# One ring of seven buffers for the experts' weights, and a new order of a short stretch of the plan

## What is computed

```
h   = x * (1 + scale1) + shift1
branches A (convolution), B (top-k attention), C (chunked gating), each projected to 1024
x   = LN(alpha*x + (1+gate1) * (merged @ w_o))
h2  = x * (1 + scale2) + shift2
scores = sigmoid(h2 @ w_router);  2 experts per token, inside one group of 4
for e in 16 experts:
    he = silu(h2 @ w_e_gate[e]) * (h2 @ w_e_up[e])      # 1024 -> 512, twice
    y += gate_e * (he @ w_e_down[e])                    # 512 -> 1024
out = LN(alpha*x + (1+gate2) * y)
```

## Time and profile before

| | us |
|---|---|
| median of 3 runs | 1103.73 |
| lowest and highest | 1097.69, 1103.95 |
| the profiled execution | 1103.72 |
| its span, first to last instruction | 1101.7 |
| PE busy | 1004.7 (91%) |
| DVE busy | 488.5 (44%) |
| mean granted TensorE clock | 0.952 |

### The profile page before, as it was taken

The page is one execution under the profiler, slowest core; times in us unless marked ns, Lnnn a source line. Parts: engine busy times, 40 slices in busy tenths (PEclk is TensorE's granted clock), DMA queues, the critical chain, the costliest instruction groups (busy, mean ns, idle before and its releaser), DMA issues. The chain is left out here.

```text
span 1101.7 us, 22153 instructions
## 1 busy us (share of the span) xinstructions
PE 1004.7 (91%) x8966; PEld 672.6 (61%) x8966; DVE 488.5 (44%) x1277; ACT 189.6 (17%) x447; POOL 247.5 (22%) x281
## 2 busy tenths in 40 slices
PE   4999999999899999999999999987999999998940
PEld 3777778456676667677777764565555555555520
DVE  1122999972357788855104005677133011110117
ACT  1110112113121213221111110111111111111103
POOL 0000004536121123222335410000221221111133
PEclk8998999999898999999999999977999999999975
DMA  9964645442514206114081317143969899999856
GB/s 293 306 124 144 196 154 173 175 159 100 212 29 153 64 29 194 31 45 115 11 199 49 115 48 306 67 181 111 354 254 414 332 375 393 419 404 423 349 151 127
DMA packets 93732, 214.23 MB, mean 194 GB/s; under 512 B 23464, under 2 KB 48303, under 8 KB 89533
## 3 DMA queue, kind: packets, MB, share of 16 engines
q1 hardware_dynamic: 78388, 186.20, 47.4%
q0 software_dynamic: 6400, 19.01, 5.8%
q10 hardware_dynamic: 8849, 7.64, 2.6%
HBM read 200.46 MB, written 16.92 MB: 197 GB/s over the span
## 5 line engine op out<-in xcount | busy, mean ns | idle before, releaser
L1765 PE MATMUL bank<-arena 128*128 128x288 f32 (+6 forms) x1778 | 443.0, 405 | 5.4 <-issue 2.1
L1765 PEld LDWEIGHTS bank<-arena 128*128 128x128 f32 (+2 forms) x1778 | 320.8, 192 | 119.5 <-issue 44.7
L2156 PE MATMUL bank<-arena 128*32 128x256 f32 x3136 | 180.6, 381 | 9.2 <-issue 7.1
L2156 PEld LDWEIGHTS bank<-arena 128*32 128x32 f32 x3136 | 102.7, 109 | 79.1 <-issue 12.3
L1717 DVE TENSOR_TENSOR arena<-arena,bank 128x128 f32<-128x128 f32 x49 | 14.2, 289 | 230.7 <-ACT arena L1154 230.5
L917 POOL DMA_INDIRECT expert_rows<-arena,ints x49 | 47.7, 974 | 228.6 <-ACT arena L1165 228.6
L2175 PE MATMUL bank<-arena 128*32 128x256 f32 x1568 | 95.8, 385 | 0.0
L867 POOL TENSOR_SCALAR arena<-arena 128x288 f32<-128x288 f32 x46 | 43.2, 938 | 209.2 <-ACT arena L1107 209.2
L1227 DVE SCALAR_TENSOR_TENSOR arena<-arena 128x512 f32<-128x512 f32 x120 | 81.9, 741 | 0.0
L1779 PE MATMUL bank<-arena 128*128 128x288 f32 x256 | 69.0, 427 | 2.6 <-DVEq L1245 2.6
L1769 PE MATMUL bank<-arena 128*128 128x128 f32 (+7 forms) x315 | 51.2, 297 | 17.3 <-DMA arena<-constants 5.3
(11 more groups left out here) (284 smaller groups left out, 891.4 us busy)
## 6 DMA issues: line engine op xcount, KB each, us to landing
arena<-in_w_e_gate SPq DMA_DIRECT2D x16, 2048.0 KB, 11.9
arena<-in_w_e_up SPq DMA_DIRECT2D x16, 2048.0 KB, 17.1
arena<-in_w_e_down SPq DMA_DIRECT2D x16, 2048.0 KB, 22.2
arena<-in_w_ada SPq DMA_DIRECT2D x8, 2048.0 KB, 10.3
arena<-in_w_in SPq DMA_DIRECT2D x8, 2048.0 KB, 10.0
arena<-in_w_ada SPq DMA_DIRECT2D x8, 1024.0 KB, 11.6
arena<-in_x_prompt SPq DMA_DIRECT2D x8, 512.0 KB, 7.3
arena<-in_w_in SPq DMA_DIRECT2D x14, 256.0 KB, 8.3
```

What stands on the lines that cost most here:

```text
L1765: last = pe.matmul(out, a, b, start=k == 0, stop=k == len(pairs_) - 1)
L2156: last = pe.matmul(out, HG[:, g % 2, k, a:a + BLK], gate_up[i % 2][:, :, k, c * P:c * P + P], start=k == 0, stop=k == KT - 1)
```

## The change

Two things change.

First, the seven buffers become one ring. Load number n = 3i + y (y = 0 gate, 1 up, 2 down) goes to slot n % 7 and may be issued when load n - 7 has been used: `room` waits for `dn_full` when that one was a down, for `hid_full` when it was a gate or up, and for `weights_up` when the slot had none. So the gate of expert i takes the slot of the down of expert i - 3, and the up and down of expert i take those of the gate and up of expert i - 2. The DMAs, their sizes and their number stay the same. The gate and up of an expert now lie any distance apart, and where up lies below gate the two halves of the PSUM bank are swapped (`gate_half`, `up_half`). Of the first loads, the down of expert 0 and the gate of expert 1 are issued where the gate and up of expert 1 were; the down of expert 1 goes early, its up late.

Second, a stretch of the plan is reordered.

```diff
-    plan += [("lnA1", 2), ("lnA2", 1), ("nat", "u", 4), ("mix", 0), ("ada", 11), ("lnA1", 3), ("lnA2", 2), ("mix", 1), ("mix", 2), ("lnA1", 4), ("lnA2", 3)]
-    plan += [("yc", 0), ("mix", 3), ("lnA2", 4), ("yc", 1), ("yc", 2)]
+    plan += [("lnA1", 2), ("lnA2", 1), ("nat", "u", 4), ("lnA2", 2), ("lnA1", 3), ("mix", 0), ("ada", 11), ("lnA1", 4), ("lnA2", 3), ("mix", 1), ("mix", 2)]
+    plan += [("lnA2", 4), ("yc", 0), ("mix", 3), ("yc", 1), ("yc", 2)]
...
-    down_ring = [ring[2], ring[5], V(A_DOWN3, SLOT)]
+    SLOT_AT = [A_RING2, A_RING2 + SLOT] + [A_RING + k * SLOT for k in range(3)] + [A_RING2 + 2 * SLOT, A_DOWN3]
+    RING = len(SLOT_AT)
+    slots = [V(a, SLOT) for a in SLOT_AT]
+    loaded = lambda n: (ev(f"w_in{n % RING}"), 16 * (n // RING + 1))
...
+    up_first = lambda i: SLOT_AT[3 * i % RING] > SLOT_AT[(3 * i + 1) % RING]
+    gate_half = lambda i: slice(P, 2 * P) if up_first(i) else slice(0, P)
+    up_half = lambda i: slice(0, P) if up_first(i) else slice(P, 2 * P)
+    def both_weights(i, k, c):
+        lo, hi = sorted((SLOT_AT[3 * i % RING], SLOT_AT[(3 * i + 1) % RING]))
+        return bass.AP(slots[0].tensor, lo + 512 * k + P * c, [[A_END, P], [hi - lo, 2], [1, P]])
+    def room(eng, n):
+        if n < RING:
+            eng.wait_ge(ev("weights_up"), 1)
+        else:
+            j, y = divmod(n - RING, 3)
+            eng.wait_ge(ev("dn_full" if y == 2 else "hid_full"), FIRST[j + 1])
...
             if t == 1:
-                expert_weights(sp, 0, 0)
-                expert_weights(sp, 0, 1)
-                expert_down(sp, 0, 0)
+                expert_weights(sp, 0, 0, 0)
+                expert_weights(sp, 0, 1, 1)
+                expert_down(sp, 1, 5)
...
         sp.wait_ge(slot_out, rel[("wo", 1)])
-        expert_weights(sp, 1, 3)
-        expert_weights(sp, 1, 4)
+        expert_down(sp, 0, 2)
+        expert_weights(sp, 1, 0, 3)
...
         sp.wait_ge(ev("rows_gathered0"), 16)
-        expert_down(sp, 1, 1)
+        expert_weights(sp, 1, 1, 4)
         sp.wait_ge(ev("order_known"), 1)
         for i in range(2, NE):
...
-            z = 3 * (i % 2)
-            sp.wait_ge(ev("hid_full"), FIRST[i - 1])
+            n = 3 * i
+            room(sp, n)
             if i == 9:
...
-            expert_weights(sp, e, z)
-            expert_weights(sp, e, z + 1)
-            if i >= 3:
-                sp.wait_ge(ev("dn_full"), FIRST[i - 2])
-            else:
-                sp.wait_ge(ev("weights_up"), 1)
-            expert_down(sp, e, i % 3)
+            expert_weights(sp, e, 0, n % RING)
+            room(sp, n + 1)
+            expert_weights(sp, e, 1, (n + 1) % RING)
+            room(sp, n + 2)
+            expert_down(sp, e, (n + 2) % RING)
...
-                    last = pe.matmul(out, HG[:, g % 2, k, a:a + BLK], gate_up[i % 2][:, :, k, c * P:c * P + P], start=k == 0, stop=k == KT - 1)
+                    last = pe.matmul(out, HG[:, g % 2, k, a:a + BLK], both_weights(i, k, c), start=k == 0, stop=k == KT - 1)
```

More of the change, by code:

```diff
@@ L357, in build_in @@
     ones = con[:, K_ONE:K_ONE + P]
-    ring = [V(a + s * SLOT, SLOT) for a in (A_RING2, A_RING) for s in range(3)]
     MG = V(A_MG, KT, NTOK)
@@ L429, in build_in @@
     YR, HEB, HETB = V(A_YR, YRS, 256), V(A_HEB, 3, P), V(A_HETB, 2, 4, BLK)
-    gate_up = [arena[:, a:a + 2 * SLOT].rearrange("p (z k n) -> p z k n", z=2, k=KT) for a in (A_RING2, A_RING)]
     GAT, BC2, OUT = V(A_GA, NT, D), V(A_BC2, 4, D), V(A_O, NT, D)
@@ L617, in build_in @@
     sp_order.sort(key=lambda x: x[0])
-    down_ring = [ring[2], ring[5], V(A_DOWN3, SLOT)]
+    SLOT_AT = [A_RING2, A_RING2 + SLOT] + [A_RING + k * SLOT for k in range(3)] + [A_RING2 + 2 * SLOT, A_DOWN3]
+    RING = len(SLOT_AT)
+    slots = [V(a, SLOT) for a in SLOT_AT]
+    loaded = lambda n: (ev(f"w_in{n % RING}"), 16 * (n // RING + 1))
+    loads_of = lambda z: len(range(z, 3 * NE, RING))
+    up_first = lambda i: SLOT_AT[3 * i % RING] > SLOT_AT[(3 * i + 1) % RING]
[10 more added lines that the diff above has]
+            eng.wait_ge(ev("dn_full" if y == 2 else "hid_full"), FIRST[j + 1])
     def expert_down(sp, e, z):
@@ L625, in expert_down, with expert_weights @@
         w = w[e] if type(e) is int else w[bass.ds(e, 1)].rearrange("e k n -> (e k) n")
-        sp.dma_start(down_ring[z].rearrange("p (k n) -> p k n", k=NJ), w.rearrange("(k p) n -> p k n", p=P)).then_inc(ev(f"down_in{z}"), 16)
-    def expert_weights(sp, e, z):
-        name, k = [("w_e_gate", KT), ("w_e_up", KT)][z % 3]
+        sp.dma_start(slots[z].rearrange("p (k n) -> p k n", k=NJ), w.rearrange("(k p) n -> p k n", p=P)).then_inc(ev(f"w_in{z}"), 16)
+    def expert_weights(sp, e, up, z):
+        name, k = [("w_e_gate", KT), ("w_e_up", KT)][up]
         w = I[name][0]
         w = w[e] if type(e) is int else w[bass.ds(e, 1)].rearrange("e k n -> (e k) n")
-        sp.dma_start(ring[z].rearrange("p (k n) -> p k n", k=k), w.rearrange("(p k) n -> p k n", p=P)).then_inc(ev(f"w_in{z}"), 16)
+        sp.dma_start(slots[z].rearrange("p (k n) -> p k n", k=k), w.rearrange("(p k) n -> p k n", p=P)).then_inc(ev(f"w_in{z}"), 16)
     @block.sync
@@ L764, in further_weights @@
             sp.wait_ge(ev("hid_full"), s + (NBLK - 1))
-            expert_weights(sp, e, 3 * p)
-            expert_weights(sp, e, 3 * p + 1)
+            expert_weights(sp, e, 0, 3 * p)
+            expert_weights(sp, e, 1, 3 * p + 1)
             sp.wait_ge(ev("dn_full"), s + (NBLK - 1))
-            expert_down(sp, e, 1 - p)
+            expert_down(sp, e, 5 - 3 * p)
+        with sp.If(nov > 0):
+            sp.wait_ge(ev("hid_full"), NBLK)
+            sp.wait_ge(ev("dn_full"), NBLK)
         each_further(sp, nov, further_weights)
@@ L1153, in _ @@
                 act.wait_ge(ev("hid_full"), b + 1)
-                act.activation(HEB[:, b % 3, :], banks[b % 3][:, 0:P], ACT.Silu).then_inc(ev("he_silu"), 1)
+                act.activation(HEB[:, b % 3, :], banks[b % 3][:, gate_half(turn_of[b])], ACT.Silu).then_inc(ev("he_silu"), 1)
             if b in tile_behind:
@@ L1716, in _ @@
                 dve.wait_ge(ev("he_silu"), b + 1)
-                tt_(HEB[:, b % 3, :], HEB[:, b % 3, :], banks[b % 3][:, P:2 * P], ALU.mult).then_inc(ev("he_ready"), 1)
+                tt_(HEB[:, b % 3, :], HEB[:, b % 3, :], banks[b % 3][:, up_half(turn_of[b])], ALU.mult).then_inc(ev("he_ready"), 1)
                 if 6 <= b < 6 + 2 * NT:
@@ L2148, in hidden @@
             if b == FIRST[i]:
-                pe.wait_ge(ev(f"w_in{3 * (i % 2)}"), 16 * (i // 2 + 1))
-                pe.wait_ge(ev(f"w_in{3 * (i % 2) + 1}"), 16 * (i // 2 + 1))
+                pe.wait_ge(*loaded(3 * i))
+                pe.wait_ge(*loaded(3 * i + 1))
             if b >= 3:
@@ L2167, in down @@
             if b == FIRST[i]:
-                pe.wait_ge(ev(f"down_in{i % 3}"), 16 * (i // 3 + 1))
+                pe.wait_ge(*loaded(3 * i + 2))
             pe.wait_ge(ev("het_up"), b + 1)
@@ L2171, in down @@
                 pe.wait_ge(ev("yo_up"), b - 1)
-            w = down_ring[i % 3].rearrange("p (k n) -> p k n", k=NJ)
+            w = slots[(3 * i + 2) % RING].rearrange("p (k n) -> p k n", k=NJ)
             for k in range(NJ):
@@ L2205, in further @@
             pe.wait_ge(ev("he_ready"), s + NBLK)
-            wg, wu = (ring[3 * p + y].rearrange("p (k n) -> p k n", k=KT) for y in range(2))
-            pe.wait_ge(ev(f"w_in{3 * p}"), 16 * i + 16 * (NE // 2 + 1))
+            wg, wu = (slots[3 * p + y].rearrange("p (k n) -> p k n", k=KT) for y in range(2))
+            pe.wait_ge(ev(f"w_in{3 * p}"), 16 * i + 16 * (loads_of(3 * p) + 1))
             group(banks[0], [(HG[:, z, k, :], wg[:, k, :]) for k in range(KT)])
-            pe.wait_ge(ev(f"w_in{3 * p + 1}"), 16 * i + 16 * (NE // 2 + 1))
+            pe.wait_ge(ev(f"w_in{3 * p + 1}"), 16 * i + 16 * (loads_of(3 * p + 1) + 1))
             group(banks[1], [(HG[:, z, k, :], wu[:, k, :]) for k in range(KT)]).then_inc(ev("hid_full"), 1)
@@ L2217, in further @@
             pe.wait_ge(ev("yo_up"), s + NBLK)
-            pe.wait_ge(ev(f"down_in{1 - p}"), 16 * i + 16 * (len(range(1 - p, NE, 3)) + 1))
-            w = down_ring[1 - p].rearrange("p (k n) -> p k n", k=NJ)
+            pe.wait_ge(ev(f"w_in{5 - 3 * p}"), 16 * i + 16 * (loads_of(5 - 3 * p) + 1))
+            w = slots[5 - 3 * p].rearrange("p (k n) -> p k n", k=NJ)
             group(banks[6], [(HET[:, p, k, :], w[:, k, 0:512]) for k in range(NJ)])
```

## The result

| | us |
|---|---|
| changed kernel, median of 6 runs | 1091.86 (1091.38 to 1096.24) |
| kernel before, median of 6 runs beside it | 1103.21 (1097.69 to 1104.96) |
| ratio, 95% interval | 0.9919 (0.9892 to 0.9947) |
| the profiled execution after, its span | 1096.24, 1094.1 |
| changed kernel measured a second time: median, ratio | 1093.91, 0.9929 (0.9901 to 0.9956) |

The change makes the kernel faster, by 8.9 and 7.8 us as the two ratios have it; both intervals leave out 1. The medians of the first measurement alone give 11.3.

What follows compares the result with a forecast made beforehand. PE, busy for 91% of the span, was taken as the bound, losing time ahead of the gates and to expert weights: 1103.7 - 7.7 - 4.8 = 1091.2 us, own range 1088 to 1094.5, 8 in 10 within 1087 to 1099.

Steps and rivals of the forecast that it cites:

- the ring's: Expert stage: earlier gate issue removes 8.7 us of weight stalls but for 1 us, a gain of 7.7 us.
- The plan's 4.8: Reordered stretch: gates begin at 286.0 at full clock, against 290.8 in effect, a gain of 4.8 us.
- The stalls of blocks 20, 26 and 30 go: Experts 6, 8 and 9: weights land before their need, so stalls of 1.02, 2.64 and 1.28 us go.
- Block 41 is left with 1 us: Expert 13: up lands at 998.9, the block would begin at 998.3; a 0.6 us wait, taken as 1.
- the chain of `BC2` and 14 matrices: DMA queue from expert 9 to up of expert 13: takes 85.7 us as before, from 913.2 to 998.9.
- over 3 us of room: Experts 5, 7 and 14: their gates wait for a later-ending down, but have over 3 us to spare.
- The wait for L1483 goes, and PE then waits for `w_pa`: Ahead of the gates: the 4.30 us wait goes; PE then waits 3.9 us for gate weights, until 286.0.
- The clock stays up in the new gap: Ahead of the gates: 3.9 us of idle leaves TensorE at full clock when the gates begin at 286.0.
- The first rival: Clock falls in the new gap ahead of the gates, costing 1.7 to 4.7 us; 1092.9 to 1095.9; chance 0.25.
- part 2: The reordered stretch of the plan ahead of the gates: its gain was put at 4.8 us.
- The other side: Hidden matmuls read halves at changing distances; 4 ns more per record cancels the gains, 15% gives 1117.6; chance 0.04.
- The gain of part 2 reaches the end: From the gates to 728 us PE is busy almost without gaps, so the whole 4.8 us carries through.

Runs made afterwards that it cites:

- ring_only: Changed kernel with the two old plan lines, so only the ring of seven buffers is new; 1098.12 us, ratio to before 0.9959.
- plan_only: Kernel before with the two new plan lines and its old buffers; 1095.79 us, ratio to before 0.9952.
- gate_held: Changed kernel with every gate also held until the hidden blocks of expert i - 2 are done; 1098.90 us, ratio to before 0.9980.
- up_first: Changed kernel with up issued ahead of the gate for experts 5, 7, 9 and 14; 1090.96 us, ratio to before 0.9910.
- bc2_late: Changed kernel with the four BC2 loads behind the last expert's loads and their DVE work moved to block 48; 1087.47 us, ratio to before 0.9883.
- ada_first: Changed kernel with the last conditioning step, ("ada", 11), moved ahead of the last u step; 1086.03 us, ratio to before 0.9840.
- six_slots: Changed kernel with a ring of six buffers, the one at A_DOWN3 left out; 1103.46 us, ratio to before 1.0004.
- before_bc2_late: Kernel before with the BC2 loads moved behind the last expert's loads and nothing else changed; 1099.53 us, ratio to before 0.9971.

## Why the prediction was right, and where not

The forecast was 1091.2 and the first measurement has 1091.86. That the two are so close is luck: the ratios put the gain at 7.8 to 8.9 us in place of 12.5, and the second measurement has 1093.91. The direction, the two mechanisms of gain and the range held. The term that was too large by the runs is the ring's: 7.7 us were forecast and `ring_only` gains 4.5, with 7.7 outside its interval. The plan's 4.8 stands against 5.3 in `plan_only`, though its clock did not stay up as forecast. Point by point:

- *The stalls of blocks 20, 26 and 30 go.* Right, by the mechanism named: `gate_held` brings them back with the old condition.
- *Block 41 is left with 1 us.* Right in kind, too small in size: 3.7. The mis-sized term is the queue at expert 9. I let the chain of `BC2` and 14 matrices start at 913.2, "which is also about when the down of expert 8 lands", 2.0 us after the issue of `BC2`. That gives 87.7 us from this issue to the landing of up 13. The runs show 997.26 - 906.34 = 90.9, and 90.4 in `ring_only`. The rate was not lower: 410 GB/s, against 411 in the 85.7 us that I took it from. So more was in the queue, about 3 us of it. It was full from 877 on, and expert 8's loads are the likely rest; their landings are not in the trace. It had also stood empty for 2.8 us ahead of 877, at the wait of expert 7's gate. The forecast looked there only at whether expert 7 itself came late ("over 3 us of room"), not at what the empty queue costs the loads behind it. `up_first` bears this out in part. PE needs 87.2 us for the same way (906.34 to 993.57), as forecast (87.1). That `bc2_late` makes the stall vanish shows that the engines' time is the bound there. The stall also lowers the clock in block 41, at 1.7 us, which the forecast had at nothing.
- *The wait for L1483 goes, and PE then waits for `w_pa`.* Right. The gates begin 12.8 us after the issue of their `w_in`, as forecast. The wait for the `mod` store, 1.44 us, was missing from the walk; it lies in front of the other and costs nothing of its own.
- *The clock stays up in the new gap.* Wrong. The first rival, put at 0.25, came true in every profile that had the gap. From the first u matmul of the last tile to the third group of gates it is 40.9 us before and 39.0 after, and 37.6 to 38.7 in the six other profiles with this gap: part 2 gains 1.9 to 3.3 us in the profiles, not 4.8. The rival's price was 1.7 to 4.7; measured are 1.6 to 3.1. Its time, 1092.9 to 1095.9, takes in the second measurement and not the first. I had weighed one stall of 3.58 idle us that left the clock alone against one gap that lowered it. Ahead of block 41, too, it is lowered in six of the eight profiles with a stall of 2.9 us or more (at 997 us in the profile after: 5.30 us for one block); that of before is one of the two where it is not.
- *The Trainium skill* (TensorE: Matmul & The Clock Gate, section "Why this matters for your kernels"), which warns of idle gaps of a few us between bursts of matmuls, named what the gap ahead of the gates then did in seven profiles of seven. Ahead of single blocks the traces are less clear-cut: idle of 2.72 us lowered the clock in `ada_first`, 3.16 (block 26, `six_slots`) and 3.60 (block 41, `gate_held`) did not. Weighing the rule by one row against it was the error.
- *The other side* (slower reads of PE across distant buffers): no sign. The median of the records of L2178 is 377 ns, which is not over the 377 that the forecast named, and their mean 382, as against 381 of L2156 before, the slow ones of block 41 included. A block takes 3.64 us in both.
- *The gain of part 2 reaches the end.* Yes: `plan_only` gains 5.3 us (3.2 to 7.4), more than the 1.9 to 3.3 that the profiles show up to the gates. The rest may be the clock elsewhere. Over whole executions the mean granted clock is 0.956 in the ten runs of `plan_only`, and 0.951 in the nineteen of the kernel before and the ten of `ring_only` on the same chip. One such fall is in the profiles, at 770 to 780 us (0.83; about 1.7 us of work): before and `ring_only` have it, the ten profiles with the new order don't, but `before_bc2_late`, with the old order, doesn't either. Where the others lie, and why the order of the plan should matter to them, no run here shows.

By the forecast's own terms the gain would be 12.5 - 2.7 (stall) - 2.3 (clock and gap, the mean of the seven profiles) = 7.5 us, and 5.8 with the clock in block 41. The ratios have 7.8 and 8.9; the 2 to 3 us between are of the size of the clock's falls elsewhere, and not shown to be these.

## What to carry to other kernels

When buffers are the limit of a prefetch, give them to the loads in the order of use: the gates issued earlier, by some 10 us at expert 8, removed three stalls of four here, with no memory and no transfer added. Then ask whether the engines have the time at all. Once the queue is full for 90 us and more, an earlier issue inside that stretch no longer helps; bytes moved out of it do, and 1.75 MB of something else can be the cheapest to move. So may a gap in the queue ahead of it that is filled. And when a wait is removed, walk on to the next wait and count its idle time for TensorE's clock as well: the gap of 4 us ahead of the dense matmuls cost another 1.6 to 3.1 us after it had ended.

## What the hardware showed that I had not expected

An idle gap of 4.0 us in two pieces, with 0.66 us of transposes between them, lowered TensorE's clock in seven profiles of seven. A single wait ahead of block 41 did so in six profiles, with 2.72 (`ada_first`) to 4.68 us of idle (`six_slots`), and left the clock alone in two, with 3.58 (before) and 3.60 (`gate_held`): the block took 5.30 us in the changed kernel and 3.66 in `gate_held`. The clock also fell without any gap: in the profile of before PE is busy throughout 770 to 780 us, at a mean clock of 0.83. The DMA engines moved 410 GB/s over 91 us beside a busy PE at full clock (87.41 us busy, clock 1.00), gathers and scatters included.
